# Start-up copies moved behind the first projection group, the first modulation block loaded in two halves, and pad slots left out of the expert scatter-add

## The chip, the cores and the metric

The kernel runs on one core of one Trainium2 chip, in float32. The metric is the device time of one execution in microseconds (us); the median of several runs counts. One further execution is recorded by the hardware profiler, and all durations below are of that one.

## The reference, cut to what matters

One layer of a streaming encoder over 1024 prompt frames and 64 sample frames, so N = 1088 rows of D = 1024:

```python
m = silu(c) @ w_ada + b_ada                 # six modulation vectors per stream
h = rmsnorm(x, g0) * (1 + sc_m) + sh_m      # first block of w_ada: sh_m, sc_m
proj = h @ w_in                             # pooling input u, q, k, v
mix = concat(pool_mixer(u), window_attention(q, k, v, sinks)) @ w_out
x = x + gt_m * rmsnorm(mix, g1)
h = rmsnorm(x, g2) * (1 + sc_f) + sh_f
scores = sigmoid(h @ w_router); sel = scores + router_bias
# 4 of 8 expert groups, then 6 of 64 experts for each row
ffn = sum over the row's 6 experts of w * swiglu(h, expert) + swiglu(h, shared)
x = x + gt_f * rmsnorm(ffn, g3)
```

Outputs are y for both streams and the new pooling and K/V caches, of which the first 64 rows of `k_s` and `v_s` are plain copies of the old caches.

## The kernel before

Each engine has its own program, and semaphores order them; the order on an engine and on a DMA queue is the order of its program. SyncE (SP) issues the large loads on one queue, GpSimd (POOL) issues small copies and all indirect DMAs on another, and both queues are served by the same 16 DMA engines.

**Start.** SP loads five small vectors, then the four 512-column parts of the first modulation block, 2 MB each (L542), with three x tiles of 512 KB behind each of the first three (L544), then w_in in three parts (L546 to L548). TensorE (PE) multiplies each part of the block with silu(c) (`ada_block`, L1474) and transposes the normalised x tiles in between (L1468). A tile is squared on ACT (L827), the root of three tiles is taken together, and VectorE (DVE) scales them (L1107). `ada_block(0)` waits for all of the first part. After the last transposes the projections begin (L1529). POOL's program begins with ten direct copies: the attention sinks twice (L690, read as single elements), the router bias and weights, the pooling history `stin`, the key cache `ckin`, two cache copies from DRAM to DRAM, and two copies of 64 x rows into rows N to N+127 of `y_acc`. It then builds constants (`ident` first) and an empty slot table of 64 x 1152 pairs in `tr`, whose 576 KB it writes to `slot_rows` (L725). `tr` also holds hT, so ACT and DVE wait for that copy (`tab_init`) before they touch x.

**Modulation rows.** During the projections DVE accumulates the other four modulation vectors from 512 KB pieces of w_ada (L564, L1171, L1174), and PE spreads each over the partitions (L1504) after every sixth projection group or so.

**Slots.** Every expert owns 1152 slots of (row, weight). A slot starts as (N + position in its tile of 128, 0). Routing scatters the real pairs into the table, and a block gather reads back the tables of the tiles in use. Each of the 83 tiles is 128 slots of one expert; 6 x 1088 = 6528 of their 10624 slots hold a row, the others are pads.

**Expert loop.** For each tile POOL gathers h2 rows (L771; its bounds check ends at N - 1 and leaves pad rows out), PE transposes them (L1749) and multiplies them with gate and up weights in three passes (L1669 to L1671), then with the down weights of the tile before (L1770). ACT scales the product with the slot weights (L1047), and POOL adds it into `y_acc` by an indirect DMA with accumulate (L779), one after the other: each waits until the one before has landed (`added`). Pads go to rows N to N+127, so all 128 rows are moved. Expert weights, 3 MB each, go through a ring of four slots (SP: L582 gate and up, L586 down). SP's loop for one expert waits until the slot is free, issues gate and up, waits for the down weights of the expert before, issues its own, waits until gate and up have landed (L663), and only then turns to the next expert. ACT rounds an arrived expert (L983), DVE forms the rest (L492), one expert ahead of PE. At the end SP reads `y_acc` back (L677) once the last scatter-add has landed, and ACT and DVE normalise and store.

Of the kernel before, what the change touches and what calls it, by code (L numbers as in the profile page):

```python
# [25 lines left out]
F32 = mybir.dt.float32  # L26
# [8 lines left out]
P = 128  # L35
D = 1024
KD = D // P
SEQ, DEC = 1024, 64
N = SEQ + DEC
NT = -(-N // P)  # L40
# [7 lines left out]
NJ = 4  # L48
KV = 128
WIN = 128  # L50
INW = PW + 512 + 2 * KV
NE, TOPK, EG, TOPG = 64, 6, 8, 4
# [10 lines left out]
CAP = NT * P  # L63
# [20 lines left out]
def build(nc, x_prompt, x_sample, c_prompt, c_sample, state_pool, cache_k, cache_v, w_ada, b_ada,  # L84
# [3 lines left out]
    with ExitStack() as ctx:  # L88
# [3 lines left out]
        def sem(name):  # L92
            return ctx.enter_context(nc.semaphore(name))
# [4 lines left out]
        slot_rows = nc.dram_tensor("slot_rows", (NE * CAP, 2), F32, kind="Internal").ap()  # L98
        y_acc = nc.dram_tensor("y_acc", (N + P, D), F32, kind="Internal").ap()

# [9 lines left out]
        tr = arena[:, BIG:BIG + TR]  # L110
# [26 lines left out]
        rec = sb("rec", [P, 16])  # L137
# [8 lines left out]
        sink = sb("sink", [P, NJ])  # L146
        wrt = sb("wrt", [P, KD, NE])
        rbias = sb("rbias", [P, NE])
# [6 lines left out]
        prod = sb("prod", [P, TOPK, NE])  # L155
# [7 lines left out]
        yw = [tr_at(2 * D, D), tr_at(3 * D, D)]  # L163
# [10 lines left out]
        def at(a, n):  # L174
            return big[:, a:a + n]

        ada = [a_.rearrange("p (k n) -> p k n", k=KD) for a_ in
               (at(0, KD * 512), at(WSLOT + KD * INW, KD * 512), at(WSLOT + KD * INW + KD * 512, KD * 512),
                xs[:, 0:KD * 512])]
# [96 lines left out]
        def bank(b):  # L276
            return ps[:, b, :]
# [5 lines left out]
        const_pool = sem("const_pool")  # L283
        small_in = sem("small_in")
        misc_in = sem("misc_in")
        ada_in = [sem(f"ada_in{s}") for s in range(4)]
        piece_in = [sem(f"piece_in{b}") for b in range(PIECES)]
# [31 lines left out]
        ev_s = sem("ev_s")  # L319
# [4 lines left out]
        pool_st = sem("pool_st")  # L324
# [47 lines left out]
        tab_init = sem("tab_init")  # L372
# [11 lines left out]
        gathered = [sem("gathered_even"), sem("gathered_odd")]  # L384
# [11 lines left out]
        added = sem("added")  # L396
# [21 lines left out]
        ada_view = w_ada[0].rearrange("(k p) n -> p k n", p=P)  # L418
# [116 lines left out]
        def _(sp):  # L535
# [5 lines left out]
            for b in range(4):  # L541
                sp.dma_start(ada[b], ada_view[:, :, 512 * b:512 * (b + 1)]).then_inc(ada_in[b], 16)  # L542
                for t in range(3 * b, min(3 * b + 3, NT)):
                    sp.dma_start(xb[t][0:ROWS[t], :], rows_of(x_prompt, x_sample, t)).then_inc(x_in[t], 16)  # L544
# [123 lines left out]
            for t in range(NT):  # L668
                if D * t % WSLOT == 0:
                    e = NE - RING + D * t // WSLOT  # L670
# [15 lines left out]
        def _(pool):  # L686
            link = chained(pool, pchain)
            for l in range(2):
                of_l = attn_sinks[0:1, :].rearrange("o (c l) -> l o c", l=2)[l]
                pool.dma_start(sink[64 * l:64 * l + 64, :], of_l.to_broadcast([64, NJ]), allow_slow_non_contiguous=True).then_inc(misc_in, 16)  # L690
            pool.dma_start(rbias[:, :], router_bias[0:1, :].to_broadcast([P, NE])).then_inc(misc_in, 16)
            pool.dma_start(wrt[:, :, :].rearrange("p k n -> p (k n)"), w_router[0].rearrange("(p k) n -> p (k n)", k=KD)).then_inc(misc_in, 16)
            pool.dma_start(stin[:, :], state_pool[0, 0]).then_inc(misc_in, 16)
            pool.dma_start(ckin[:, :], cache_k[0, 0].rearrange("s h d -> s (h d)")).then_inc(misc_in, 16)
            pool.dma_start(k_s[0, 0, 0:DEC], cache_k[0, 0, DEC:WIN]).then_inc(pool_st, 16)
            pool.dma_start(v_s[0, 0, 0:DEC], cache_v[0, 0, DEC:WIN]).then_inc(pool_st, 16)

            for r in (0, P // 2):
                pool.dma_start(y_acc[N + r:N + r + P // 2, :], x_prompt[0, r:r + P // 2, :]).then_inc(added, 16)
            link(pool.memset(ident[:, :], 0.0))  # L700
# [8 lines left out]
            low = dict(allow_small_or_imprecise_dtypes=True)  # L709
            pool.iota(pcol[:, :], [[0, 1]], base=0, channel_multiplier=1, **low)  # L710
            pool.iota(iotae[:, :], [[1, NE]], base=0, channel_multiplier=0, **low)
            pool.iota(rec[:, :], [[1, 16]], base=1, channel_multiplier=0, **low)
            link(pool.memset(lower8[:, :, :], 1.0))
# [5 lines left out]

            blank = tr[0:NE, 0:2 * CAP].rearrange("p (t r c) -> p t r c", t=NT, c=2)  # L720
            link(pool.memset(blank, 0.0))
            pool.iota(blank[:, :, :, 0], [[0, NT], [1, P]], base=N, channel_multiplier=0, **low)\
                .then_inc(const_pool, 1)
            pool.wait_ge(const_pool, 2)
            pool.dma_start(slot_rows.rearrange("(e r) c -> e (r c)", e=NE), tr[0:NE, 0:2 * CAP]).then_inc(tab_init, 16)  # L725

            pool.wait_ge(ada_mm, 4)
            pool.memset(u[:, :, 0:HIST], 0.0).then_inc(uz_s, 1)


# [12 lines left out]
            for t in range(NT):  # L743
                r, c = slice(0, ROWS[t]), t // (SEQ // P)
# [20 lines left out]

            gather_bound, add_bound = pool.to_reg(N - 1), pool.to_reg(N + P - 1)

            def gather(i, b):
                pool.wait_ge(idx_s, i + 1)
                pool.sem_inc(pool_turn, 1)  # L770
                pool.indirect_dma_start(out=xg[b], out_offset=None, in_=h2_rows,  # L771
                                        in_offset=bass.IndirectOffsetOnAxis(ap=idxg[b][:, 0:1], axis=0),
                                        bounds_check=gather_bound, oob_is_err=False).then_inc(gathered[b], 16)

            def scatter_add(i, b):
                pool.wait_ge(added, 16 * (i + 2))
                pool.wait_ge(yw_s, i + 2)
                pool.sem_inc(pool_turn, 1)
                pool.indirect_dma_start(out=y_acc, out_offset=bass.IndirectOffsetOnAxis(ap=idxs[b][:, 0:1], axis=0),  # L779
                                        in_=yw[b], in_offset=None, bounds_check=add_bound,  # L780
                                        compute_op=ALU.add).then_inc(added, 16)
# [5 lines left out]
                                    in_=slot_rows.rearrange("(j s) c -> j (s c)", s=P),  # L787
                                    in_offset=bass.IndirectOffsetOnAxis(ap=blocks[:, 0:1], axis=0),
# [25 lines left out]
        def _(act):  # L814
# [25 lines left out]

            act.wait_ge(tab_init, 16)
            act.wait_ge(ms_s, 1)
# [242 lines left out]
        def _(dve):  # L1085
# [22 lines left out]

            dve.wait_ge(tab_init, 16)
            dve.memset(maskb[:, :, :], 0.0)  # L1110
# [343 lines left out]
        def _(pe):  # L1454
# [16 lines left out]
            def ada_block(b):  # L1471
                pe.wait_ge(ada_in[b], 16)
                for k in range(KD):
                    ins = pe.matmul(bank(b)[0:2, :], sil[:, k, :], ada[b][:, k, :], start=(k == 0), stop=(k == KD - 1))  # L1474
                ins.then_inc(ada_mm, 1)
# [14 lines left out]

            pe.wait_ge(misc_in, 16 * 6)
            pe.wait_ge(ht_s, NT - len(ACT_TILES))
# [119 lines left out]
            pe.wait_ge(o_s, NCH)  # L1612
            pe.wait_ge(w_out_s, 48)

            def mix(t, between):
# [207 lines left out]
```

## Time and profile before

| | |
|---|---|
| median of 3 runs | 1466.43 us (1465.84 to 1475.8) |
| profiled execution, its own time | 1465.69 us |
| span of its profile | 1463.9 us |
| mean granted TensorE clock | 0.977 of full speed |
| busy: PE, DVE, ACT, POOL | 91%, 54%, 45%, 26% of the span |
| DMA moved | 352.38 MB, 241 GB/s over the span |

The profiled execution lies 0.74 us under the median. The time from the span's end points to the execution's own time is 1.8 us. Busy shares are averages over stages with different limits: the start (0 to 63 us), the projections and attention (to 306 us), output projection, routing and shared expert (to 564 us), the expert loop (to 1424 us) and the ending.

### The profile page before, as it was taken

How to read it: one execution, taken by the hardware profiler on the slowest of the kernel's cores; microseconds unless marked ns; L12 is line 12 of the kernel's file. 1: busy time of each engine (PE TensorE's matmuls, PEld its weight loads, DVE VectorE, ACT ScalarE, POOL GpSimd, SP SyncE). 2: the span in 40 equal slices, each digit the busy share in tenths (PEclk: the TensorE clock that was granted, in tenths of full speed). 3: DMA queues.
4: the chain of work that ended last, by engine and by line, in shares of the span. 5: the costliest groups of instructions: out<-in, count | busy, mean ns of one | idle time of the engine just before them, and what ended most of it. 6: DMA issues, size and time to landing. Idle time of an engine off the chain costs nothing.

```text
span 1463.9 us, 22685 instructions
## 1 busy us (share of the span) xinstructions
PE 1338.2 (91%) x5590; PEld 882.4 (60%) x5591; DVE 794.7 (54%) x1254; ACT 656.7 (45%) x916; POOL 387.2 (26%) x274
## 2 busy tenths in 40 slices
PE   4999997899998989999999999999999999999950
PEld 1467654545455766766666666776667667667630
DVE  2446676835887634555546454465545345555426
ACT  2300005734435335555555454465555345555523
POOL 3000000003565431233333323243222333232330
PEclk9999999999999999999999999999999999999995
DMA  8925424032221626999999999999999989999977
GB/s 303 347 79 184 143 69 120 1 145 86 87 90 42 223 88 227 343 324 322 358 310 307 349 318 358 295 311 326 362 324 317 261 225 275 290 338 322 315 193 254
DMA packets 106744, 352.38 MB, mean 241 GB/s; under 512 B 16369, under 2 KB 18517, under 8 KB 106356
## 3 DMA queue, kind: packets, MB, share of 16 engines
q1 hardware_dynamic: 79864, 279.39, 52.8%
q0 software_dynamic: 26560, 72.38, 21.3%
q8 instruction: 19, 0.31, 0.1%
q10 hardware_dynamic: 284, 0.16, 0.1%
q14 instruction: 17, 0.14, 0.0%
HBM read 307.15 MB, written 62.83 MB: 253 GB/s over the span
## 4 chain that ended last, share of the span: by engine, by line
PE 39%; DMA 37%; DVE 9%; SPq 5%; issue 4%; ACT 3%; POOL 2%; ACTq 0%; POOLq 0%; DVEq 0%
DMA raw<-in_w_up_dram 25%; DMA y_acc<-arena,idxs 8%; PE ps L1529 7%; PE ps L1770 7%; PE ps L1669 4%; PE ps L1671 4%; PE ps L1670 4%; SPq L582 3%; PE ps L1622 3%; DMA arena<-in_w_ada_dram 2%; PE ps L1474 2%; DMA y_acc<-arena 2%; PE ps L1749 2%; SPq L649 1%; PE ps L1534 1%
## 5 line engine op out<-in xcount | busy, mean ns | idle before, releaser
L492 DVE TENSOR_TENSOR lo_ring<-raw,hi_gate_up (+1 forms) x128 | 287.7, 2289 | 166.5 <-ACT hi_gate_up L983 156.6
L1770 PE MATMUL ps<-raw,aT 128*128 x664 | 301.9, 598 | 19.3 <-ACT aT L1042 17.0
L983 ACT ACTIVATE hi_gate_up<-raw (+1 forms) x128 | 238.1, 1908 | 120.4 <-SPq L663 93.5
L779 POOL DMA_INDIRECT y_acc<-arena,idxs x83 | 152.2, 1834 | 522.8 <-DMA y_acc<-arena,idxs 389.6
L1669 PE MATMUL ps<-hi_gate_up,xTh 128*128 x664 | 266.3, 401 | 1.1 <-issue 1.1
L1671 PE MATMUL ps<-hi_gate_up,xTl 128*128 x664 | 259.5, 391 | 0.0
L1670 PE MATMUL ps<-lo_ring,xTh 128*128 x664 | 259.0, 390 | 0.0
L1770 PEld LDWEIGHTS ps<-raw,aT 128*128 128x128 f32 x664 | 120.2, 191 | 142.9 <-issue 142.8
L771 POOL DMA_INDIRECT arena<-h_rows,idxg x86 | 114.8, 1334 | 100.0 <-DVE idxg L1407 77.0
L1671 PEld LDWEIGHTS ps<-hi_gate_up,xTl 128*128 128x128 f32 x664 | 124.7, 188 | 26.9
L1669 PEld LDWEIGHTS ps<-hi_gate_up,xTh 128*128 128x128 f32 x664 | 124.8, 188 | 24.5 <-issue 1.2
L1670 PEld LDWEIGHTS ps<-lo_ring,xTh 128*128 128x128 f32 x664 | 125.0, 188 | 23.7
L1398 DVE TENSOR_TENSOR xTl<-ps,xTh 128x1024 fp32r<-128x1024 f32 x84 | 102.7, 1223 | 66.4 <-ACT xTh L1002 66.2
L1529 PE MATMUL ps<-arena 128*128 128x384 f32 (+1 forms) x432 | 135.8, 476 | 1.1 <-DVE arena L1138 1.1
L1622 PE MATMUL ps<-arena 128*128 128x512 f32 (+1 forms) x288 | 128.4, 601 | 0.5 <-ACT arena L910 0.5
L1389 DVE TENSOR_TENSOR arena<-arena,ps 128x256 f32<-128x256 f32 x83 | 34.8, 419 | 166.7 <-ACT arena L1062 166.6
L1047 ACT ACTIVATE arena<-ps,wcol 128x1024 f32<-128x1024 f32 x83 | 91.3, 1100 | 58.9 <-PE ps L1770 44.3
L1062 ACT ACTIVATE arena<-ps 128x256 f32<-128x256 f32 x82 | 31.4, 383 | 189.4 <-PE ps L1671 189.3
L1529 PEld LDWEIGHTS ps<-arena 128*128 128x128 f32 x432 | 83.2, 193 | 53.0 <-issue 5.0
L750 POOL TENSOR_TENSOR arena<-arena 128x1024 f32<-128x1024 f32 (+1 forms) x9 | 22.0, 2443 | 314.8 <-DVE arena L1305 314.8
L1002 ACT ACTIVATE xTh<-ps 128x1024 fp32r<-128x1024 f32 x84 | 86.1, 1025 | 33.4 <-PE ps L1749 33.3
L1622 PEld LDWEIGHTS ps<-arena 128*128 128x128 f32 (+1 forms) x288 | 52.4, 186 | 65.4 <-issue 64.5
(244 smaller groups left out, 1457.4 us busy)
## 6 DMA issues: line engine op xcount, KB each, us to landing
raw<-in_w_gate_dram SPq DMA_DIRECT2D x128, 512.0 KB, 6.0
raw<-in_w_up_dram SPq DMA_DIRECT2D x128, 512.0 KB, 9.0
raw<-in_w_down_dram SPq DMA_DIRECT2D x64, 1024.0 KB, 11.8
arena<-in_w_ada_dram SPq DMA_DIRECT2D x32, 512.0 KB, 6.4
arena<-in_w_ada_dram SPq DMA_DIRECT2D x4, 2048.0 KB, 17.4
arena<-in_x_prompt_dram SPq DMA_DIRECT2D x16, 512.0 KB, 8.9
x_rows<-arena SPq DMA_DIRECT2D x8, 512.0 KB, 2.9
h_rows<-arena SPq DMA_DIRECT2D x8, 512.0 KB, 2.6
```

What stands on the lines that cost most here:

```text
L492: return eng.tensor_tensor(lo_of(e, m), raw_of(e, m), hi_of(e, m).bitcast(F32), ALU.subtract)
L771: pool.indirect_dma_start(out=xg[b], out_offset=None, in_=h2_rows, in_offset=bass.IndirectOffsetOnAxis(ap=idxg[b][:, 0:1], axis=0), bounds ...
L779: pool.indirect_dma_start(out=y_acc, out_offset=bass.IndirectOffsetOnAxis(ap=idxs[b][:, 0:1], axis=0), in_=yw[b], in_offset=None, bounds_c ...
L983: act.activation(hi_of(e, m), raw_of(e, m), ACT.Copy).then_inc(round_gu, 1)
L1047: act.activation(yw[b], pair(2), ACT.Copy, scale=wcol[b][:, 0:1]).then_inc(yw_s, 1)
L1398: dve.tensor_tensor(xTl, pair(6).rearrange("p (k n) -> p k n", k=KD), xTh.bitcast(F32), ALU.subtract)\
L1529: ins = pe.matmul(out[:, 0:n_], w1[:, k, P * c:P * (c + 1)], hT[:, k, a:a + n_], start=(k == 0), stop=(k == KD - 1))
L1622: ins = pe.matmul(bank(2 * (t % 2) + half)[0:ROWS[t], :], hT[:, k, P * t:P * t + ROWS[t]], wo[:, k, 512 * half:512 * half + 512], start=(k ...
L1669: pe.matmul(out, at_h[:, k, :], w_h, start=first, stop=False)
L1670: pe.matmul(out, at_h[:, k, :], w_l, start=False, stop=False)
L1671: return pe.matmul(out, at_l[:, k, :], w_h, start=False, stop=last)
L1770: ins = pe.matmul(bank(2 + half), aT[:, k, :], down[:, k, 512 * half:512 * half + 512], start=(k == 0), stop=(k == KF - 1))
```

## The change

- POOL's program begins with `stin` and `ckin` alone. The sinks, router bias, router weights and cache copies are issued after the first projection group has left PSUM (`ev_s` at 1), behind the slot table.
- The empty table is built once for 128 slots in `prod` and written nine times by one DMA with a repeated source (64 x 9 runs of 1 KB). ACT and DVE wait for it no more. PE waits for two copies in place of six before it transposes the histories, and for all six before the output projection.
- The first part of the modulation block is loaded in two halves of 1 MB with a semaphore each, and PE starts on the first.
- `y_acc` has N + 2 rows in place of N + 128, and two copies of one row stand for the two of 64. The scatter-add's bounds check ends at N - 1 without an error, so pad slots are out of bounds.

```diff
-        y_acc = nc.dram_tensor("y_acc", (N + P, D), F32, kind="Internal").ap()
+        y_acc = nc.dram_tensor("y_acc", (N + 2, D), F32, kind="Internal").ap()
...
             for b in range(4):
-                sp.dma_start(ada[b], ada_view[:, :, 512 * b:512 * (b + 1)]).then_inc(ada_in[b], 16)
+                cols_b = slice(512 * b, 512 * (b + 1))
+                if b == 0:
+                    sp.dma_start(ada[b][:, 0:KD // 2, :], ada_view[:, 0:KD // 2, cols_b]).then_inc(ada_first, 16)
+                    sp.dma_start(ada[b][:, KD // 2:KD, :], ada_view[:, KD // 2:KD, cols_b]).then_inc(ada_in[b], 16)
+                else:
+                    sp.dma_start(ada[b], ada_view[:, :, cols_b]).then_inc(ada_in[b], 16)
...
             link = chained(pool, pchain)
-            for l in range(2):
-                of_l = attn_sinks[0:1, :].rearrange("o (c l) -> l o c", l=2)[l]
-                pool.dma_start(sink[64 * l:64 * l + 64, :], of_l.to_broadcast([64, NJ]), allow_slow_non_contiguous=True).then_inc(misc_in, 16)
-            pool.dma_start(rbias[:, :], router_bias[0:1, :].to_broadcast([P, NE])).then_inc(misc_in, 16)
-            pool.dma_start(wrt[:, :, :].rearrange("p k n -> p (k n)"), w_router[0].rearrange("(p k) n -> p (k n)", k=KD)).then_inc(misc_in, 16)
             pool.dma_start(stin[:, :], state_pool[0, 0]).then_inc(misc_in, 16)
             pool.dma_start(ckin[:, :], cache_k[0, 0].rearrange("s h d -> s (h d)")).then_inc(misc_in, 16)
-            pool.dma_start(k_s[0, 0, 0:DEC], cache_k[0, 0, DEC:WIN]).then_inc(pool_st, 16)
-            pool.dma_start(v_s[0, 0, 0:DEC], cache_v[0, 0, DEC:WIN]).then_inc(pool_st, 16)
-
-            for r in (0, P // 2):
-                pool.dma_start(y_acc[N + r:N + r + P // 2, :], x_prompt[0, r:r + P // 2, :]).then_inc(added, 16)
...
-            blank = tr[0:NE, 0:2 * CAP].rearrange("p (t r c) -> p t r c", t=NT, c=2)
+            blank = prod[0:NE, :, :].rearrange("p k e -> p (k e)")[:, 0:2 * P].rearrange("p (r c) -> p r c", c=2)
             link(pool.memset(blank, 0.0))
-            pool.iota(blank[:, :, :, 0], [[0, NT], [1, P]], base=N, channel_multiplier=0, **low)\
-                .then_inc(const_pool, 1)
-            pool.wait_ge(const_pool, 2)
-            pool.dma_start(slot_rows.rearrange("(e r) c -> e (r c)", e=NE), tr[0:NE, 0:2 * CAP]).then_inc(tab_init, 16)
+            link(pool.iota(blank[:, :, 0], [[1, P]], base=N, channel_multiplier=0, **low))

             pool.wait_ge(ada_mm, 4)
             pool.memset(u[:, :, 0:HIST], 0.0).then_inc(uz_s, 1)
+
+            pool.wait_ge(ev_s, 1)
+            pool.dma_start(slot_rows.rearrange("(e t r) c -> e t (r c)", e=NE, t=NT),
+                           blank.rearrange("p r c -> p (r c)").unsqueeze(1).to_broadcast([NE, NT, 2 * P])).then_inc(tab_init, 16)
...
+            for r in range(2):
+                pool.dma_start(y_acc[N + r:N + r + 1, :], x_prompt[0, r:r + 1, :]).then_inc(added, 16)
...
-                                        in_=yw[b], in_offset=None, bounds_check=add_bound,
+                                        in_=yw[b], in_offset=None, bounds_check=row_bound, oob_is_err=False,
                                         compute_op=ALU.add).then_inc(added, 16)
...
-            act.wait_ge(tab_init, 16)
...
-            dve.wait_ge(tab_init, 16)
...
-                pe.wait_ge(ada_in[b], 16)
+                pe.wait_ge(ada_first if b == 0 else ada_in[b], 16)
                 for k in range(KD):
+                    if b == 0 and k == KD // 2:
+                        pe.wait_ge(ada_in[b], 16)
...
-            pe.wait_ge(misc_in, 16 * 6)
+            pe.wait_ge(misc_in, 16 * 2)
...
             pe.wait_ge(w_out_s, 48)
+            pe.wait_ge(misc_in, 16 * 6)
```

The copies of the sinks, `rbias`, `wrt`, `k_s` and `v_s` that are taken out around `stin` and `ckin` stand again, unchanged and in that order, between the new write of the slot table and the two row copies.

## Rows read from the trace of the kernel before

**Rows 1.** The page: shares of the chain that ended last, by engine.
```profile
PE 39%; DMA 37%; DVE 9%; SPq 5%; issue 4%; ACT 3%; POOL 2%; ACTq 0%; POOLq 0%; DVEq 0%
```

**Rows 2.** That chain in order of time, 0 to 500 us: start, us, what.
```profile
2.78 17.13 DMA arena<-in_w_ada_dram
20.05 9.14 PE ps L1474 x16
29.19 1.90 PE ps L1468 x16
...
43.06 13.82 PE ps L1474 x32
...
62.69 32.48 PE ps L1529 x96
95.16 3.43 PE ps L1504 x8
```

**Rows 3.** That chain in the expert loop, 470 us to the end.
```profile
608.76 9.09 DMA raw<-in_w_up_dram
...
741.97 12.13 DMA raw<-in_w_up_dram
...
1042.99 0.87 PE ps L1749 x8
...
1223.11 0.87 PE ps L1749 x8
```

**Rows 4.** Windows: length, busy PE, PEld, DVE, ACT, POOL, clock, DMA share, GB/s.
```profile
574.70:1398.40 823.70, 806.08 (x3362) 563.13 (x3361) 423.98 (x524) 442.59 (x444) 256.01 (x160) 1.00 0.98 315
574.80:725.20 150.40, 141.96 (x591) 98.55 (x589) 82.80 (x96) 83.14 (x82) 48.95 (x28) 1.00 1.00 334
```

**Rows 5.** PE's groups, 574.7 to 1398.4 us: busy, mean ns, idle before.
```profile
L1749 PE MATMUL ps<-ident,arena 128*128 128x128 f32 x640 | 82.8, 272 | 0.0
```

**Rows 6.** Timeline of the ending, 1396 to 1440 us.
```profile
1411.63 3.69 PE L1770 MATMUL ps<-raw,aT 128*128 x8 [1.65 <-issue]
1416.27 0.15 DVE L1402 COPY wcol<-maskb 128x1 f32 x1 [8.73 <-DMA y_acc<-arena,idxs]
...
1424.03 1.55 POOL L779 DMA_INDIRECT y_acc<-arena,idxs  x1 [5.64 <-issue]
```

**Rows 7.** DMA issues of the whole span: KB, us to landing.
```profile
arena<-in_w_out_dram SPq DMA_DIRECT2D x1, 2048.0 KB, 8.1
```

**Rows 8.** DMA of 0 to 20 us: packets, MB, share; KB, us to landing.
```profile
q0 software_dynamic: 448, 1.57, 34.1%
...
sink<-in_attn_sinks_dram POOLq DMA_DIRECT2D x2, 1.0 KB, 6.3
```

**Rows 9.** Windows of half a microsecond at the start, columns as in rows 4.
```profile
5.50:6.00 0.50, 0.00 (x0) 0.00 (x0) 0.00 (x0) 0.00 (x0) 0.50 (x2) 1.00 0.00 0
...
8.50:9.00 0.50, 0.00 (x0) 0.00 (x0) 0.12 (x1) 0.22 (x1) 0.50 (x5) 1.00 0.95 365
```

**Rows 10.** Timeline of 0 to 70 us.
```profile
8.65 0.22 ACT L817 ACTIVATE sil<-colv 128x16 f32<-128x16 f32 x1 [6.58 <-DVE colv L1092]
...
23.84 1.06 ACT L827 ACTIVATE arena<-arena 128x1024 f32<-128x1024 f32 x1 [0.15 <-DMA arena<-in_x_prompt_dram]
...
26.75 2.08 DVE L1107 TENSOR_SCALAR arena<-arena,rstd 128x1024 f32<-128x1024 f32 x3
```

**Rows 11.** Landing time of the fourth modulation part, whose issue began at 31.16 us.
```profile
DMA to landing us min/median/max: 17.7/17.7/17.7
```

**Rows 12.** Timeline of DVE, 62 to 130 us.
```profile
69.22 16.83 DVE L1174 SCALAR_TENSOR_TENSOR arena<-arena,sil 128x1024 f32<-128x1024 f32 x14
```

**Rows 13.** DMA of 574.7 to 1398.4 us, columns as in rows 8.
```profile
q1 hardware_dynamic: 51793, 192.13, 63.1%
q0 software_dynamic: 22775, 66.93, 34.7%
...
y_acc<-arena,idxs POOLq DMA_INDIRECT x80, 9.7
```

## The prediction before the change was run

> **What bounds the kernel now.** I began with the chain that ended last. By engine it is shared between PE and DMA [rows 1], so neither one nor the other bounds the whole; it has to be read in order of time. At the start it is one load: the first 2 MB of the modulation block, issued at 2.78 and landed at 19.91, then PE without a gap of note, and the projections from 62.69 [rows 2]. In the expert loop the chain changes between two faces [rows 3]. From 608.76 to 741.97 it runs through the weight loads, eleven steps of 12.11 us, one per expert. From 1042.99 to 1223.11 it is PE alone: 18 tiles, 10.007 us each. The window over the loop [rows 4] says what the first face costs: with 640 / 8 = 80 tiles in 823.7 us [rows 4, 5], 80 x 10.007 = 800.6 would do, so 23.1 us are waits for weights. In the first run of loads (574.8 to 725.2) PE was idle for 150.40 - 141.96 = 8.4 us of them [rows 4]. The last scatter-add is a third place: PE's last product is done at 1415.32, but the add goes out at 1424.03, because the one before it had not landed [rows 6].
>
> **The start.** The load took 17.13 us. A first load of the same size on queues that stood idle landed in 8.1 [rows 7]. What lay in between is POOL's: 6.8 us of all 16 engines (34.1% of 20) for 1.57 MB [rows 8], and something that these shares do not show. From 5.5 to 6.0 no byte moved and at 8.5 the rate was full [rows 9], while SP's load had been issued since 2.78. The two 1 KB sink copies took 6.3 us to land, in just that time [rows 8]. I read this as SP's packets standing behind their single elements on every engine. The change takes the sinks and all but 94 KB of POOL's copies out of this stretch.
> The sum: 2.78 + 8.1 = 10.9 for the whole part, 9.0 earlier. Its first half, with 1 MB at the 365 GB/s of [rows 9] less, lands about 8.0. PE needs silu(c) too, done at 8.87 [rows 10]; with eight of ten issues gone ahead of `ident` on POOL it cannot be later. So PE starts near 8.9, 11.1 earlier, and its 9.14 us run to 18.0; the second half is there by 10.9. Then x decides. The third x tile landed at 23.8; the first scaling by DVE began at 26.75 and its first tile of three takes 0.7 [rows 10], 3.7 us after that landing. All of x is behind the part in the same queue, so 9.0 earlier: 14.8 + 3.7 = 18.5, and the transposes begin at 18.6 in place of 29.19 [rows 2]: 10.6 gained. Later loads bound this once more: the fourth part landed at 31.16 + 17.7 = 48.9 [rows 11], now 39.9, and PE comes to it at 43.06 + 6.9 - 10.6 = 39.4 [rows 2]: 0.5 of wait. I take **10 us**. If nothing were late it would be 11.1. If the late first packet is not the sinks' doing, only POOL's engine time goes, nearly 6.8: 6 us is the other end. I take the value near the upper end because the idle-queue load of [rows 7] is the same size and direction. The split adds one issue on SP, some 0.4 us for what is behind it, which is inside that rounding. The waits of ACT and DVE for the table lay ahead of x's landing and gave nothing by themselves.
>
> **What is moved behind the first group.** The table, six copies and two row copies are now issued when PE has finished one projection group. On POOL nothing waits behind them until the residual adds of the output projection; sinks are read in attention, router inputs after it, the old caches not at all. Their cost is the DMA time, again up to 6.8 us, beside DVE's modulation pieces. DVE ends the first eight at 69.22 + 16.83 = 86.05 [rows 12], and PE asks for them at 95.16 [rows 2]: 9.1 us of cover, so I cost it at 0. Were the cover gone it could be 0 to 7; nothing there can gain. The later three blocks have little cover, but their pieces come when these copies have long landed. PE's wait for all six copies before the output projection is over some 240 us earlier.
>
> **The pads.** In the loop's window [rows 13] the direct queue moved 192.13 MB in 63.1% of 823.7 = 519.8 us, 2.71 us per MB. The indirect queue took 34.7% = 285.8 us for 66.93 MB. Its 80 scatter-adds of 128 rows of 4 KB are 41.94 MB, so the gathers moved 25.0 MB in place of 41.9: the gather's bounds check does leave 4140 pads untransferred, which is the row for what the scatter-add will do. Gathers at the direct price are 67.7 us, so the scatter-adds took 218.1, 2.73 us each or 21.3 ns a row, twice a plain row's price. 4140 rows less are 88 us of 16 engines, **1.10 us per tile**. It fits: weights 3.15 MB x 2.71 = 8.5, gather 0.85 and scatter-add 2.73 make 12.1 for an expert of one tile, which is the 12.11 of SP's loop. There DMA has no time left (share 1.00, [rows 4]).
> Not all of it need arrive. Pads are the last slots of a tile, and if fixed engines serve fixed slots, the engines of the first slots keep their work, while a weight load is spread over all 16 and lands with the slowest. No row shows which engine served which slot. Full relief brings an expert to 10.98, half to 11.53. I take 0.8: 11.28. The Trainium skill (DMA: Bandwidth & Descriptors, "The descriptor swizzle") gives partitions 0 to 63 of a 128-partition transfer to engines 0 to 7 and the others to 8 to 15. By that the pads would nearly all lie with the upper half, and the gain of this part would be at the half-relief end; no run here shows it for an indirect DMA.
> What the stalls become: in the first run eleven loads lost 11 x 2.1 = 23.1 us against PE's 10.0, and PE waited only 8.4 of them, so it had 14.7 us of lead. At 11.28 the loss is 14.1: no wait. The other 23.1 - 8.4 = 14.7 us come after pauses of unknown lead; by proportion (1.28 / 2.1) at most 9.0 stay, and with some lead few. I leave 5 and gain **18 us**; full relief would give up to 23, half relief with no lead at all (2.1 + 10.7 left) 10.
> The ending: PE's end 1415.32, a short copy, ACT's scaling 1.1, issue: 1417.0 in place of 1424.03 [rows 6]. The scatter-adds' lag of 7 us should drain, since each lands sooner; I take **6.5**, between 3 (tiles full to the last slot land no sooner) and 7.
>
> **The sum.** 10 + 18 + 6.5 = 34.5. The profiled execution took 1465.7, 1.8 of it outside its span, and lies 0.7 under the median, so 1431.2 there and **1432** as a median.
>
> **Rivals.**
> *Half relief or less.* Fixed engines keep the rows of the low slots. For it: pads always lie at the top. Against: even so the upper engines become free earlier, and some small tiles empty low slots as well. Loop gain 10 to 16, ending 5, start 10: 1437 to 1441.
> *The first load stays late.* The queue needs its 5 us to the first packet whatever POOL does. For it: the idle stretch at 5.5 itself, in which no engine was busy with the sinks either. Against: 8.1 us in [rows 7]. Start gain 6: 1436.
> *Leaving rows out saves no DMA time with an accumulate,* so only the start gains: 1456. Against: the gather's 25.0 MB.
> *Slower.* Place: the chain of scatter-adds, one at a time on POOL. It was 9.7 us from issue to landing [rows 13], with the next issue some 0.6 later about the pace of the tiles (823.7 / 80 = 10.3). If POOL paid for each left-out row, 50 per tile, the chain would bound the loop. It decides from 10.5 us a link, where it has eaten the start and the ending too; with 10.3 - 1.1 as the base that is 26 ns a row. At 50 ns: 11.7 a link, 80 x 1.2 = 96 us over the present time, 1560. Against: the gather leaves out as many on the same engine and keeps up.
>
> **Chances.** Forecast, 1425 to 1435: 0.46. Half relief 0.26, late first load 0.18, no saving 0.06, slower 0.04. The range reaches from all upper ends (11.1 + 23.1 + 7 = 41: 1425, one less for rounding) to all lower ones (6 + 10 + 3 = 19: 1447). Faster by over 1%, under 1451.8, are the first three and part of the spread of the fourth: 0.91; within 1%, which is about what a measurement of this kernel can tell from no change: 0.05; slower 0.04.
>
> **What would show it.** The first load in halves landing near 8 and 11 us, the projections at 52 to 53; the indirect queue near 50 MB in the loop; the chain on PE from some 600 us on, idle PE in the loop's window at a third of 17.6 us or less, and the last scatter-add about 2 us after PE's last product. It is wrong if the first packet still starts at 7.5, if weight loads still take 12 us a step with 17 MB less to move, or if the modulation pieces stretch past PE's demand.

## The result, and the profile after

The kernel after took 1451.81 us as a median of five executions (1444.77 to 1454.91), the kernel before on the same chip 1468.3: a ratio of 0.9896 (95% interval 0.9869 to 0.9924), so 16 us or 1% faster. Timed again on another chip: 1449.98 against 1466.16, 0.9892 (0.9858 to 0.9927). The forecast was 1432 with 1447 as the upper end of its range: the sign was right, and less than half of the gain came.

The profiled execution is the fastest of the five (1444.77, span 1442.8), so the difference of the two spans, 21.1 us, is on the large side. By place it falls into 11.8 us ahead of the loop, 4.0 in it and 5.2 behind it (to the nearest tenth; the loop is counted from the third tile to the last, as in [rows 4]).

The chain that ended last, in order of time (start, us, what):

```profile
21.81 18.05 DMA arena<-in_w_ada_dram
39.90 7.04 PE ps L1481 x16
...
48.87 9.82 DMA arena<-in_w_ada_dram
62.55 14.10 DMA arena<-in_w_ada_dram
84.08 3.67 PE ps L1511 x8
87.75 29.25 PE ps L1536 x96
...
608.39 8.59 DMA raw<-in_w_up_dram
619.84 8.83 DMA raw<-in_w_up_dram
...
732.62 11.15 DMA raw<-in_w_up_dram
...
1402.71 6.09 DMA y_acc<-arena,idxs
```

Read it beside [rows 2, 3]. Ahead of the loop the fourth modulation block sets the time, as forecast, and PE is done with it at 46.94 where before it was 56.88: 9.9 earlier. In the loop the chain still runs through the loads of the up weights, and from 608.39 to 732.62 there are ten steps of 12.42 us. Before there were eleven of 12.11. The step that was to fall to 11.28 did not fall at all.

Windows over the loop and over its first run of loads, columns as in [rows 4]:

```profile
562.96:1382.57 819.61, 804.37 (x3363) 562.34 (x3361) 423.21 (x524) 442.70 (x444) 258.36 (x161) 1.00 0.92 299
```
```profile
563.00:713.40 150.40, 142.83 (x595) 99.32 (x594) 82.74 (x96) 84.25 (x83) 49.80 (x29) 1.00 0.95 317
```

The DMA share fell from 0.98 to 0.92, and from 1.00 to 0.95 in the first run, and PE's idle time there only from 8.4 to 7.6 us. The queues of the same stretch, columns as in [rows 13]:

```profile
q1 hardware_dynamic: 52294, 193.93, 66.2%
q0 software_dynamic: 22968, 51.28, 25.9%
...
y_acc<-arena,idxs POOLq DMA_INDIRECT x80, 9.4
```

The pads did what they were to do for the indirect queue: 51.28 MB in place of 66.93, and 25.9% of 819.6 = 212 us of all 16 engines in place of 286. So 74 us of engine time were freed, of the 88 that were forecast, and 4 arrived. The direct queue took part of it: 66.2% of 819.6 = 543 us in place of 520 for 1% more bytes, 2.80 us per MB in place of 2.71. The ending, to be read beside [rows 6]:

```profile
1394.92 3.69 PE L1778 MATMUL ps<-raw,aT 128*128 x8 [0.81 <-ACT aT L1048]
...
1402.71 1.56 POOL L786 DMA_INDIRECT y_acc<-arena,idxs  x1 [5.72 <-issue]
```

From PE's last product (1398.61) to the last scatter-add it is now 4.1 us; it was 8.7.

### The profile page after: what moved, and what is told of

Read it like the earlier page. It is cut to its first block, busy times and chain, and to the rows that moved or that the text cites. A ratio compares the mean times of both kernels' runs of the same rounds, so it can differ in the third digit from the quotient of the medians.

```text
span 1442.8 us, 22685 instructions
## 1 busy us (share of the span) xinstructions
PE 1338.2 (93%) x5590; PEld 882.9 (61%) x5591; DVE 794.4 (55%) x1254; ACT 656.7 (46%) x916; POOL 386.9 (27%) x274
## 4 chain that ended last, share of the span: by engine, by line
PE 49%; DMA 27%; DVE 10%; SPq 5%; issue 4%; ACT 3%; POOL 1%; ACTq 0%; POOLq 0%; DVEq 0%
DMA raw<-in_w_up_dram 19%; PE ps L1778 11%; PE ps L1677 7%; PE ps L1679 7%; PE ps L1678 7%; PE ps L1536 5%; DMA arena<-in_w_ada_dram 3%; PE ps L1630 3%; PE ps L1757 3%; SPq L588 3%; DMA y_acc<-arena,idxs 2%; DMA raw<-in_w_down_dram 2%; DVE arena L1179 1%; SPq L550 1%; PE ps L1541 1%
## 5 line engine op out<-in xcount | busy, mean ns | idle before, releaser
L1778 PE MATMUL ps<-raw,aT 128*128 x664 | 300.2, 595 | 16.1 <-ACT aT L1048 10.8
L786 POOL DMA_INDIRECT y_acc<-arena,idxs x83 | 169.1, 2037 | 465.0 <-DMA y_acc<-arena,idxs 283.8
L778 POOL DMA_INDIRECT arena<-h_rows,idxg x86 | 100.0, 1163 | 143.3 <-DVE idxg L1412 118.0
## 6 DMA issues: line engine op xcount, KB each, us to landing
raw<-in_w_down_dram SPq DMA_DIRECT2D x64, 1024.0 KB, 11.5
```

What stands on the lines that cost most here:

```text
L1778: ins = pe.matmul(bank(2 + half), aT[:, k, :], down[:, k, 512 * half:512 * half + 512], start=(k == 0), stop=(k == KF - 1))
```

## The experiments

The measure of the loop in what follows is its length from the first gate product of the third tile to that of the last, 80 tiles, less 80 x 10.005 us = 800.4, the pace of PE alone: 823.65 - 800.4 = 23.3 before, 819.61 - 800.4 = 19.2 after. I call it the excess. A second profile of the kernel before gave 24.6, and five profiles of the loop of the kernel after (two of itself, three of kernels that share it) gave 18.8 to 23.2 (all below), so a difference of 4 us between two profiles says little.

Two theories stood against one another for the lost gain. **A, the gap:** SyncE asks for the next expert's gate and up weights only when the last ones have landed; the freed time lies between a landing and the first packets of the next load, where weights can't use it. **B, fixed engines:** a slot of a tile is served by a fixed DMA engine; pads are the upper slots, so the engines of the lower slots have as much to do as before, and a load spread over all 16 lands with the slowest. B was the forecast's first rival, there with half of the gain.

Half a microsecond at a time, the traces don't rule out either. The kernel before, around two loads (same columns):

```profile
656.50:657.00 0.50, 0.50 (x2) 0.19 (x1) 0.50 (x3) 0.50 (x1) 0.00 (x0) 1.00 0.46 180
657.00:657.50 0.50, 0.50 (x2) 0.19 (x1) 0.19 (x4) 0.50 (x1) 0.45 (x1) 1.00 0.33 123
```
```profile
670.00:670.50 0.50, 0.50 (x4) 0.38 (x3) 0.00 (x0) 0.50 (x1) 0.20 (x2) 1.00 0.30 82
670.50:671.00 0.50, 0.50 (x4) 0.42 (x3) 0.00 (x0) 0.50 (x2) 0.50 (x1) 1.00 0.61 90
671.00:671.50 0.50, 0.50 (x4) 0.42 (x3) 0.21 (x1) 0.50 (x1) 0.36 (x1) 1.00 0.92 172
671.50:672.00 0.50, 0.50 (x4) 0.42 (x3) 0.50 (x1) 0.50 (x1) 0.00 (x0) 1.00 1.09 188
```

At these two loads the engines stood up to two thirds idle, inside a stretch whose mean share is 1.00; and the window with 1.09 moved 188 GB/s, little more than half of the stretch's mean of 334 [rows 4], so a share near one is no proof that bytes move at the full rate. They are the exception before: at the other ten loads issued from 607 to 741 us the share stays at 0.86 or more, while the rate falls to between 189 and 254 GB/s, as at the load issued at 618.85:

```profile
618.50:619.00 0.50, 0.50 (x4) 0.42 (x3) 0.00 (x0) 0.50 (x1) 0.00 (x0) 1.00 1.09 229
```

In the kernel after idle engines are the rule: ten of the eleven loads issued from 606 to 732 us have a half microsecond at a share of 0.66 or less. One of them, with SyncE's issues in the same place:

```profile
667.50:668.00 0.50, 0.50 (x4) 0.41 (x3) 0.00 (x0) 0.47 (x1) 0.00 (x0) 1.00 0.48 116
668.00:668.50 0.50, 0.50 (x3) 0.39 (x3) 0.00 (x0) 0.50 (x1) 0.00 (x0) 1.00 0.43 123
...
669.00:669.50 0.50, 0.50 (x4) 0.42 (x3) 0.00 (x0) 0.50 (x2) 0.00 (x0) 1.00 0.43 107
```
```profile
668.70 0.86 SPq L588 DMA_DIRECT2D raw<-in_w_gate_dram  x2
669.66 0.86 SPq L588 DMA_DIRECT2D raw<-in_w_up_dram  x2
```

And the queues from 667.5 to 669.5:

```profile
q0 software_dynamic: 141, 0.14, 33.8%
q1 hardware_dynamic: 32, 0.12, 14.5%
```

With the weights' queue nearly empty, what was under way of gathers and scatter-adds took a third of the engines' time: the next load could have used the rest (A), and the third may be a few engines with many rows (B).

**The two halves of the change, each alone.** To the kernel before: (1) the new start alone; (2) the new bound alone.

```
(1) kernel after, but
-  y_acc (N + 2, D); row_bound in the scatter-add
+  y_acc (N + P, D); add_bound = N + P - 1 in the scatter-add
(2) kernel before, but
-  bounds_check=add_bound
+  bounds_check=gather_bound, oob_is_err=False
```

(1) 

> This is the kernel before with the start of the kernel after (copies moved behind the first projection group, slot table written once and broadcast, first modulation block in two halves); the 128 pad rows of the accumulator stay and every pad slot is still added into them. If the start is worth what the two profiles show, every stage from the projections on comes 11.7 us earlier and the rest is as before: about 1456 us where the kernel before has 1468. Rival: the loop gives part of it back, because the pad traffic that fills the loop doesn't care when it begins; then 1460 to 1468 with the first gate/up tile still 11 to 12 us earlier.

(2) 

> This is the kernel before with one edit: rows past the last token are left out of the scatter-add. If the loop and the ending are worth what the two profiles show (loop 3.9 us, ending 5.5 us), about 1459 us where the kernel before has 1468, with the load step at 12.1 to 12.4 us. If the small gain in the loop of the kernel after came from its earlier start and not from the pads themselves, the loop alone gains the forecast 18 us here: about 1444.

Measured (1): 1458.62 against 1463.91, 0.9972 (0.9943 to 1.0), 4 us by the ratio (0 to 8) where some 12 were expected. Its profile, like that of the kernel after, has the loop 8.9 us earlier than before, and its length is unchanged, excess 23.0:

```profile
565.89:1389.31 823.42, 806.53 (x3363) 563.38 (x3362) 423.89 (x524) 442.44 (x444) 254.10 (x161) 1.00 0.99 316
```

So the loop gives nothing back, but the size of the start is less clear by the timed runs than by the profiles. Over all profiles here the loop begins at 562.9 to 568.3 us in the ten with the new start, one of them without the split (mean 565.2), and at 572.3 to 576.3 in the six with the old one (574.6): 9.4 us between the means. Measured (2): 1459.61, 0.9962 (0.9938 to 0.9987), 5.6 us. The loop starts where it did before; its excess is 18.8:

```profile
574.67:1393.89 819.22, 804.18 (x3364) 562.79 (x3362) 423.15 (x524) 442.23 (x444) 262.93 (x161) 1.00 0.92 299
```

So the 18 us that were forecast for the loop are not there without the new start either, at a DMA share of 0.92 as in the kernel after.

**An earlier issue (theory A).** Only the place of one wait of SyncE changes:

```
 load_gate_up(g, s)
+sp.wait_ge(gu_slot[of the expert before], ...); sp.sem_inc(gu_ready, 1)
 sp.wait_ge(dn_slot[of the expert before], ...); sp.sem_inc(dn_ready, 1)
 sp.wait_ge(dn_mm, last_of + 1)
 load_down(g, s)
-sp.wait_ge(gu_slot[s], g * 64 + 64); sp.sem_inc(gu_ready, 1)
```

> The kernel after, with one edit on SyncE: the gate and up loads of the next expert are issued before the wait for the landing of this one, so that the queue never runs dry. Theory A (the time that the pads freed lies in the gap between a landing and the first packet of the next load): the step falls from 12.4 to about 11.4 us and the loop gains 9 to 19 us, 1433 to 1443 where the kernel after has 1452. Theory B (slots are served by fixed DMA engines, the pads sit in the upper slots, so the engines of the lower slots carry what they carried before and a load lands with the slowest of them): those engines have no free time, so 0 to 4 us, 1448 to 1452.

Measured: 1437.55, 0.9814 (0.9775 to 0.9852) of the kernel before, where the kernel after has 0.9892: 11 us faster. Excess 11.5:

```profile
564.44:1376.30 811.86, 802.98 (x3364) 562.28 (x3362) 423.22 (x524) 443.81 (x444) 245.71 (x161) 1.00 0.91 302
```

That is more than B allowed. The late issue costs.

**Spread slots (theory B).** After the slot table is read, four copies on GpSimd reorder the slots of every tile, the same in its gathers, weights and scatter-adds. Which engine serves a slot no row names. The Trainium skill (DMA: Bandwidth & Descriptors, "The descriptor swizzle") gives, for a plain transfer to 128 partitions, engine = 8 x (partition >> 6) + ((partition >> 2) & 7). No run here shows it directly for an indirect one; the runs below fit it, and the new order of the slots follows it.

```
+for c in range(2):
+    for h in range(2):
+        ins = pool.tensor_copy(tabp[:, c, 64 * h:64 * h + 64].rearrange("p (a b d) -> p a b d", a=2, b=8),
+                  tabr[:, :, c].rearrange("p (a d h b) -> p h a b d", a=2, d=4, h=2)[:, h])
-pe.transpose(..., tabr[:, :, c], ident)
+pe.transpose(..., tabp[:, c, :], ident)
```

> The kernel after, with one edit: the slots of each tile are reordered after the slot table is read (four small copies on GpSimd), so that each 16 rows of a tile in order of rank lie on 16 different DMA engines if engine = 8 for the upper 64 partitions plus bits 2 to 4 of the partition. The rows of a tile, and the skipped pads, are the same in number. Theory B (the freed time is on engines that were not the slowest): scatter-adds and gathers of a half-full tile now use all engines, a step falls from 12.4 to 11.3 to 11.6 us, and the loop gains 10 to 18 us: 1434 to 1442 where the kernel after has 1452. Theory A (the queue runs dry between a landing and the next load): the gap is as long as before, so -3 to +2 us: 1449 to 1454.

Measured: 1434.48, 0.9787 (0.9749 to 0.9825) of the kernel before: 15 us under the kernel after. Its loop begins 5.1 us later than there, inside the spread of the new start given above; its excess is 5.2:

```profile
568.07:1373.62 805.55, 801.88 (x3363) 562.58 (x3362) 423.66 (x524) 444.10 (x444) 261.44 (x161) 1.00 0.94 304
```

That is more than A allowed. Neither theory alone holds: the late issue and the order of the slots each hold the loads up. A control with the same copies, but only the halves of 64 slots exchanged (one execution):

```
+        ins = pool.tensor_copy(tabp[:, c, 64 * h:64 * h + 64], tabr[:, 64 * (1 - h):64 * (1 - h) + 64, c])
```

> A control for the spread slots: the kernel after with the slots of each tile reordered by the same four copies, but only the two halves of 64 swapped, so that the low ranks lie on the upper 64 partitions. If what the spread gave comes from the use of all 16 engines, this gives nothing: the excess over 10.005 us a tile stays where the kernel after has it (19 to 23 us). If it came from the reordering as such, the copies, or rows that no longer follow one another, the excess falls towards the 5.2 us of the spread.

Measured: 1453.83 in its one execution, excess 26.2, more than the 19 to 23 named and far from 5.2. By the formula other engines get the rows, as few as before, and nothing is gained:

```profile
564.92:1391.52 826.60, 808.43 (x3363) 564.18 (x3362) 423.09 (x524) 443.07 (x444) 252.18 (x161) 0.99 0.92 297
```

The exchange keeps most neighbouring rows together, so by itself it doesn't exclude that the order of the rows matters, whatever engine moves them. The times from issue to landing in the loop speak to that. The spread slots:

```profile
arena<-h_rows,idxg POOLq DMA_INDIRECT x81, 7.5
y_acc<-arena,idxs POOLq DMA_INDIRECT x80, 8.6
```

In the kernel after they are 8.6 for the gathers and 9.4 for the scatter-adds, with the halves exchanged 8.8 and 9.4. Where all 128 rows are added, the spread should then quicken the gathers alone, and it does: with the early issue and the pads added (both below) they are 9.1 and 9.1 with slots in order, and spread:

```profile
arena<-h_rows,idxg POOLq DMA_INDIRECT x81, 7.9
y_acc<-arena,idxs POOLq DMA_INDIRECT x80, 9.1
```

The scatter-add's rows are put in the same new order, and with all of them moved it gains nothing. That speaks for rows spread over the engines and against the order as such.

**Both, and each in the kernel before,** beside the kernel after again. The edits are those above.

Kernel after again: 

> The kernel after itself, timed again beside the kernel before on the chip of these runs, as the mark for the other three: 0.99 of the kernel before (1449 where that has 1464). Its start (11.7 us in the profiles) and its pads (loop 4, ending 5.5) should add up to more than the 4 us that each gave alone by the medians of the runs before; if they don't, 1454 to 1456.

Both in the kernel after: 

> The kernel after with both edits: next gate and up loads issued before the wait for the last landing, and the slots of a tile spread over all 16 DMA engines. Over 10.005 us for each of the 80 tiles the kernel after loses 19.2 us in its profile, with the early issue 11.5, with the spread slots 5.2. If the two take away different idle time (a gap between loads, and engines that end late), 0 to 2 us are left: 3 to 5 us under the spread slots alone, about 1430. If they take away the same idle time, 1434 as with the spread slots alone.

Spread in the kernel before: 

> The kernel before (every pad slot still added into a pad row) with the slots of each tile spread in the same way. All 128 slots are moved either way, so the scatter-add is the same for every engine; only the gathers, which left pads out before too, become even. Theory B (the spread pays because the pads left out are spread): the excess over 10.005 us a tile falls from 23.3 us to 19 to 23, time 1460 to 1464. Rival (the gathers' unevenness, or the order of the rows itself, was the cost): it falls by the 14 us of the kernel after, 1450.

Early issue in the kernel before: 

> The kernel before with the next gate and up loads issued before the wait for the last landing. If the gap between loads was filled with pad traffic there (DMA share 1.00 of the stretch to 725 us), an earlier issue has no free time to use: 0 to 3 us, 1461 to 1464, and the excess over 10.005 us a tile stays at 20 to 23 us. If the gap costs in itself, whatever else is queued, it gains the 8 us that it gave in the kernel after: 1456.

Both in the kernel before: 

> The kernel before, all pad slots still added, with both edits in the loop: gate and up loads of the next expert issued before the wait for the last landing, and the slots of each tile spread over the 16 DMA engines. With the same two edits the kernel after loses 0.1 us over 10.005 us a tile, so what this one loses is what leaving the pads out is worth once nothing else holds the loads up. Alone the edits left 12.3 us (spread) and 6.7 us (early issue) here. If the pads' DMA time is then the limit, 3 to 7 us stay, 1435 to 1442 by the start and ending of the kernel before; if the loads have room even with the pads, 0 to 2 us stay, 1432 to 1436.

Early issue in the kernel after, pads added again: 

> The kernel after with the early issue of the gate and up loads, but with the pad slots added into pad rows again (128 rows in each scatter-add), so that it differs from the kernel with the early issue alone by the pads only. If leaving pads out always relieves the loads, the loop is slower than the 11.5 us of that one: 14 to 20 us of excess. If with slots in order of rank it relieves only engines that are not the slowest, the excess is the same within 3 us. In the kernel before the same edit left 6.7 us: if that is no accident, leaving pads out costs the loop 5 us here, and the excess is 6 to 8 us.

| slots, issue of loads | pads added: ratio to before, excess | pads left out: ratio to before, excess |
|---|---|---|
| in order, late | 1, 23.3 (again: 24.6); new start: 0.9972, 23.0 | 0.9962, 18.8; new start: 0.9892, 19.2 (again: 22.3) |
| in order, early | 0.9859, 6.7; new start: 0.9802, 8.7 | new start: 0.9814, 11.5 (again: 10.8) |
| spread, late | 0.9907, 12.3 | new start: 0.9787, 5.2 |
| spread, early | 0.9819, 0.1 | new start: 0.9732, 0.2 |

The rows of four of them: the kernel after again, spread in the kernel before, early issue in the kernel before, and both in the kernel after.

```profile
562.92:1385.67 822.75, 807.22 (x3364) 563.57 (x3362) 423.25 (x524) 443.05 (x444) 255.48 (x161) 1.00 0.92 298
```
```profile
573.70:1386.44 812.74, 805.07 (x3364) 562.95 (x3362) 422.95 (x524) 443.75 (x444) 245.33 (x160) 1.00 0.99 319
```
```profile
572.29:1379.42 807.13, 802.29 (x3363) 562.30 (x3362) 427.19 (x524) 445.49 (x444) 273.61 (x161) 1.00 0.98 323
```
```profile
568.29:1368.84 800.55, 800.55 (x3364) 562.01 (x3362) 424.67 (x524) 445.63 (x444) 261.30 (x161) 1.00 0.93 306
```

The kernels of the two start experiments (below) have the loop of the kernel after, slots in order and late: 23.2 and 20.9. With both edits no load holds PE up, whether pads are added or not. The kernel after with both took 1426.95 against 1466.16, 0.9732 (0.9704 to 0.976), the fastest version here. The row that settles most is that of the kernel before with both edits, all pads added:

```profile
575.98:1376.49 800.51, 800.51 (x3363) 562.69 (x3362) 424.22 (x524) 445.22 (x444) 226.16 (x161) 1.00 0.99 326
```
```profile
575.98:726.40 150.42, 150.42 (x635) 105.80 (x634) 85.84 (x101) 89.09 (x88) 41.99 (x31) 1.00 1.04 361
```

It moves every byte of the kernel before, and PE doesn't wait once. In the first run of loads 361 GB/s went through, where the kernel before moved 334 at the share of 1.00 that I had read as full [rows 4]. SyncE's issues of the eleven loads that were 12.11 us apart in the kernel before are 11.42 us apart here:

```profile
597.32 0.85 SPq L583 DMA_DIRECT2D raw<-in_w_gate_dram  x2
...
722.92 0.85 SPq L583 DMA_DIRECT2D raw<-in_w_gate_dram  x2
```

Two of the expectations fell outright. The spread was to give next to nothing in the kernel before, since 128 rows are added either way; it gave 11 us of excess. The gathers left their pads out before too, and by the landing times above they are the part that the reordering changed. The early issue was to find no time in the kernel before, or 8 us at the most; it took 16.6 off the excess. Idle gaps were rare there, so a closed gap alone doesn't explain this. What the rows do show is that a weight load's price moves. The direct queues with both edits, first with the pads added, then with them left out:

```profile
q1 hardware_dynamic: 52218, 193.69, 62.4%
q1 hardware_dynamic: 52250, 193.82, 65.8%
```

Over loops of 800.5 us that is 2.58 and 2.72 us per MB, where the kernels before and after have 2.71 and 2.80. With the early issue alone it is 2.59 in the kernel before. So the early issue goes with cheaper weight loads, and leaving the pads out with dearer ones; why was not found.

Two further executions, with no edit new:

Early issue in the kernel after, again: 

> The kernel after with the early issue again, for its loop: 11.5 us of excess in its first profile, while the two profiles with the same early issue and the pads kept have 6.7 and 8.7. If leaving the pads out costs the loop something there, 11 to 13 us again; if these are the same within what one profile varies, 6 to 9.

Kernel before, again: 

> The kernel before again, for what one profile of it varies: 23.3 us of excess over 10.005 us a tile in the loop and 25.6 us from the start of the last tile to the issue of its scatter-add in the first. If the ending's gain of 5.5 us belongs to the pads, this is 24 to 27 us again; the kernel with the new start alone, pads kept, showed 20.9, by which it can be 20 to 22.

The early issue has 10.8 us of excess again, against 6.7 and 8.7 with the pads added. So with slots in order leaving the pads out may have cost the early loop some 3 us, which is not clear of what profiles vary; by the ratios (0.9802 with pads, 0.9814 without) it gained nothing in all. The kernel before has 24.6, and 24.2 us from the start of its last tile to the issue of that tile's scatter-add, 25.6 in its first profile; the kernel after has 20.1.

**The start, in pieces,** one execution each: the first modulation block in one piece again, and the copies of sinks, router bias and router weights at the front again.

```
(1) -  two halves, PE waits for ada_first, then for ada_in[0]
    +  one load, PE waits for ada_in[0]
(2) +  the four copies ahead of state_pool on POOL, as before; PE waits for all six before the transposes
```

(1) 

> The kernel after with the first modulation block loaded and waited for in one piece, as before. In the kernel after the half lands at 8.2 us and the whole at 10.9 us, but the fourth block lands at 39.9 us and the work behind it starts then: by that row the split gives nothing past the fourth block, and the first projection group starts within 0.5 us of that of the kernel after. Rival: the early start of the first transposes and copies keeps the later ones from piling up behind the fourth block; then it starts 1 to 3 us later.

(2) 

> The kernel after with the copies of the sinks, the router bias and the router weights issued first of all again, as before; the slot table, the pad rows and the cache copies stay where the change put them. If the element-wise sink copies hold up the first loads of SyncE, the first modulation block lands about 4 us later and the fourth 4 to 6 us later. If it was the bytes of the slot table and the pads (0.87 MB, some 2.5 us at 350 GB/s), the first lands within 1 us and the fourth 1 to 2.5 us later.

The chains, (1) and then (2), the lines that answer to 21.81 and 39.90 of the kernel after:

```profile
21.84 18.20 DMA arena<-in_w_ada_dram
40.08 7.04 PE ps L1475 x16
```
```profile
28.70 18.08 DMA arena<-in_w_ada_dram
46.83 7.03 PE ps L1481 x16
...
59.66 30.98 PE ps L1536 x96
90.64 3.43 PE ps L1511 x8
```

The split is worth 0.2 us past the fourth block. The four copies are worth 46.83 - 39.90 = 6.9 of the 9.9 us, more than the 4 to 6 expected; their first half-block landed 11.1 us after its issue, where it is 5.4 in the kernel after. By difference some 2.8 are left for the slot table, the pad rows and the cache copies.

## Why the prediction was wrong

**The loop term failed,** and with it the sum. The step in words of the prediction: weights 8.5, gather 0.85 and scatter-add 2.73 "make 12.1 for an expert of one tile, which is the 12.11 of SP's loop. There DMA has no time left". From that it took 0.8 of the 1.10 us freed per tile off each step. The prediction's own sign of being wrong came: loads that still take 12 us a step, 12.42 in fact. The agreement of the two 12.1 didn't show a limit. The kernel before with both edits moves the same bytes in steps of 11.42 us, and no tile waits. Two things held the loads up that are not in this sum. One is their late issue, which stands in no term and no rival of the prediction (shown: the early issue takes 16.6 us of excess away in the kernel before, 8 to 11.5 in the kernel after). The other is the order of the slots (shown: the spread takes 11 and 14 to 17, the exchange of halves nothing); it acts, by the reading that fits, through the engines that had most rows. Nor was the price of a weight load fixed, as the sum had it: it rose from 2.71 to 2.80 us per MB, so that 23 of the 74 us freed went to the direct queue, and much of the rest shows as idle engines around the landings. The excess fell from 23.3 to 19.2, or by 3.2 between the means of the two profiles of each (24.0 and 20.8), in place of the forecast 18.

**The first rival had a mechanism that fits, and the wrong price.** Fixed engines were weighed, for half of the relief; 10 to 16 us of gain stayed in it. That the place of a slot decides who moves its row is supported by the reorderings and the landing times; the engine itself no row names. With it the pads are worth 7 us of the loop once the slots are spread (12.3 to 5.2, one profile each), little that can be told from no gain while they are in order, and nothing once the loads are issued early too (0.1 and 0.2). The upper engines "become free earlier", which I had counted for the relief, was worth little; that a load waits for the lower ones is the reading that fits.

**The start was right:** 10 us forecast, 9.9 at the end of the modulation, 11.8 at the loop in the first two profiles and 9.4 over all. Its steps came as forecast too: the fourth block landed at 39.9 and the projections began at 52.73. In the timed pairs that differ by the start alone it was 4 (0 to 8), 8 and 10 us, by the ratios of the table. Its larger part is that of the copies, as argued; whether the sinks' single elements or the two other inputs did it was not separated. The cover of the moved copies was used up, which I had costed at nothing with 9.1 us to spare: the modulation pieces issued at 62.55 landed 14.10 later, beside these copies, and PE's next step came at 84.08, right behind DVE. With four of the copies at the front that step follows the modulation's end by 36.8 us (53.86 to 90.64); by that it would have been at 83.7. But it follows by 36.8 to 39.0 us in the ten profiles with the new start and by 36.8 to 38.3 in the six with the old one, so no price is clear of the spread.

**The ending came near its number,** 5.2 us of the forecast 6.5, but the reason given, that each scatter-add lands sooner without its pads, is not shown. Four kernels that still add them, the one with the new start, the two with the early issue and the one with both edits, have 19.3 to 20.9 us from the last tile's start to its scatter-add, against 24.2 and 25.6 in the kernel before, 23.5 with its slots spread, and 20.1 in the kernel after. So luck may have a part in it. The lag at the end depends on what the loop left.

The other rivals: the first load did not stay late, rows left out of an accumulate do save DMA time (51.28 MB, 212 us), and POOL pays nothing that matters for them (9.4 us from issue to landing, 9.7 before).

**Open.** Why direct packets take longer without the pads, and whether the early loop really loses some 3 us more without them, was not found. The early issue also gives a lead of one more expert; how much of its gain is the lead, how much the closed gap and how much the cheaper loads was not separated.

## What to carry to other kernels

A DMA share near one over a long window doesn't show that bandwidth is the limit. Look at it in half-microsecond pieces around each landing, at the bytes per second beside it, and at who issues the next load and when. Bytes taken off a queue gave little here while the loads waited for something else: before skipping work in a transfer whose rows lie in order, spread what remains over the engines, and issue the next load before waiting for the last.

## What was not expected of the hardware

The busy share of the DMA engines goes over one: 1.09 in a half microsecond at 188 GB/s, 1.04 over 150 us at 361. The order of the slots in a tile, with the same rows and bytes, was worth 14 us of a loop of 820, by gathers and scatter-adds of 4 KB rows that take a quarter of the engines' time. A row left out of a scatter-add freed its own time, but the direct packets beside it took longer: 2.80 us per MB for 2.71 with late issue, 2.72 for 2.58 with both edits.
